# Delta rule units: inverse and masked blocks in the other half of the partitions, both updates' products in turn

## The chip, the core and the metric

The kernel runs on one core of one Trainium2 chip. A core has a matrix engine (TensorE, PE in the profile, with its weight loads as PEld), VectorE (DVE), ScalarE (ACT), GpSimd (POOL) and SyncE (SP), which issues the DMAs here. Each engine works through its own queue in order, and semaphores tie the queues together. The metric is the device time of one execution in microseconds (us), the median of several.

## What is computed

The reference runs two kinds of transformer blocks, two layers of each, on 512 tokens of width 1024, all in float32. What matters here is the delta rule of the first kind: 8 heads, chunks of 64 tokens, in both directions of time. For each head, direction and chunk it inverts a unit triangular 64x64 matrix:

```python
decay = jnp.exp(jnp.where(incl, gcum[..., :, None] - gcum[..., None, :], -jnp.inf))
k_beta = k * beta[..., None]
a_kk = jnp.where(strict, jnp.einsum("bhnid,bhnjd->bhnij", k_beta, k) * decay, 0.0)
eye = jnp.eye(c, dtype=q.dtype)
t_inv = lax.linalg.triangular_solve(eye + a_kk, jnp.broadcast_to(eye, a_kk.shape),
                                    left_side=True, lower=True, unit_diagonal=True)
u = jnp.einsum("bhnij,bhnjd->bhnid", t_inv, v * beta[..., None])
w = jnp.einsum("bhnij,bhnjd->bhnid", t_inv, k_beta * jnp.exp(gcum)[..., None])
```

A scan over the 8 chunks then carries a 64x64 state per head. Around it lie projections, grid attention, gates and a feed-forward network; the second kind of block has three other attention branches.

## The kernel before

The program is written five times over, once for each engine (classes Tensor, Scalar, Vector, Pool, Sync), with methods of the same names. Each method is a generator; `mixed` interleaves the generators in a fixed order, so that each engine's queue holds the delta rule's steps with other work (attention, projections, gates: the fill) between them. `up` marks a step as done on a semaphore, `at` names it for a wait. PSUM has eight banks, handed out in turn by `take` and put back by `give`, which says which steps must be over before the next user.

The delta rule's work is cut into units (l, g, jp, r): layer, group of four heads, pair of heads, direction. The two directions r = 0 and r = 1 run abreast, so a block (l, g, jp) holds two units, and there are eight blocks. A unit covers two heads and eight chunks, which is sixteen 64x64 matrices. They lie in tiles of 128 partitions by 512 elements: chunk parity a picks the partition half (64a to 64a + 63), and (head, pair of chunks) picks one of eight column blocks. Each r has five such tiles of s_xb: X, Y, Pm, A, AT.

TensorE's `eight` (L608) forms sixteen products of 64x64, one for each a and column block; half a of the operands gives half a of the result. `mm` (L517) is the line under which nearly all matmuls appear. A float32 product shows as two matmuls.

A unit runs as follows (Tensor L885, Vector L2252, Pool L2682).

- Gates, the products k k and q k (L915), masks; VectorE forms A (L2277) and the masked q k (L2282).
- TensorE transposes A to AT (L923), ScalarE copies it to s_xb.
- GpSimd masks: Pm from A (step X1, L2699), block C(1) from AT (L2705), Y from AT (step Y1, L2708), then C(2) to C(5), each one round ahead of its use. The C lie in three s_tmp tiles.
- VectorE forms the first inverse X = I - Pm (L2286) and its transpose Y = I - Y (L2288).
- Rounds b = 1 to 5 double the size of the inverted blocks: P = C x X on TensorE (L932), copied by ScalarE to Pm; then, for b < 5, all sixteen products of X's update (L939), then the sixteen of Y's (L942); VectorE subtracts each from X and Y (L2297, L2303). Round 5 updates Y only.
- u and w (L947 to L955): u = Y x value rows, w = A x Y. In w and in the products k k and q k the two inner loops run over all four pairings of an operand half with a result half.

On TensorE a round is: P of r = 0, P of r = 1, a step of fill or none, X and Y of r = 0, X and Y of r = 1, a step of fill or none. After both blocks of a group comes the chain over the chunks.

Of the kernel before, what the change touches and what calls it, by code (L numbers as in the profile page):

```python
# [37 lines left out]
M_ID = 14  # L38
# [74 lines left out]
def v8(a):  # L113
    return a.rearrange("p (b n) -> p b n", b=8)
# [399 lines left out]
class Tensor(Program):  # L514
# [90 lines left out]
            last = self.e.transpose(ps[:, i * 128:(i + 1) * 128], src[:, i * 128:(i + 1) * 128], self.m.cst[:, K_ID, :])  # L605
        return last

    def eight(self, ps, left, right):  # L608

        for b in range(8):  # L610
            for a in range(2):
                pr, s = slice(64 * a, 64 * a + 64), slice(b * 64, (b + 1) * 64)
                last = self.mm(ps[pr, s], left[pr, s], right[pr, s] if right is not None else self.m.cstm[pr, M_ID, :], True, True)
        return last

# [266 lines left out]

    def unit(self, l, g, jp, r):  # L885

        m, sc = self.m, self.m.sc
        X, Y, Pm, A, AT = m.slot[r]
        key, both = (l, g, jp, r), (l, g, jp)
# [30 lines left out]
        yield  # L920
        ps = self.take((key, "AT"))
        self.w.wait_ge(*self.at("vec_unit", key, "A", 1))
        self.eight(ps, A, None).then_inc(*self.up("pe_unit", key, "AT"))  # L923
        self.give((key, "AT"), ("act_unit", key, "AT"))
        yield
        yield
        for b in range(1, 6):
            C = self.tmp((key, "C", b))
            ps = self.take((key, "P", b))
            self.w.wait_ge(*self.at("pool_unit", key, "C", b))  # L930
            self.w.wait_ge(*self.at("vec_unit", key, "X", b - 1))
            self.eight(ps, C, X).then_inc(*self.up("pe_unit", key, "P", b))  # L932
            self.give((key, "P", b), ("act_unit", key, "P", b))
            yield
            self.w.wait_ge(*self.at("act_unit", key, "P", b))
            self.w.wait_ge(*self.at("vec_unit", key, "Y", b - 1))
            if b < 5:
                ps = self.take((key, "X", b))
                self.eight(ps, Y, Pm).then_inc(*self.up("pe_unit", key, "X", b))  # L939
                self.give((key, "X", b), ("vec_unit", key, "X", b))  # L940
            ps = self.take((key, "Y", b))
            self.eight(ps, Pm, Y).then_inc(*self.up("pe_unit", key, "Y", b))  # L942
            self.give((key, "Y", b), ("vec_unit", key, "Y", b))
            yield
        ps = self.take((key, "u"))
# [1001 lines left out]
class Vector(Program):  # L1947
# [304 lines left out]
    def unit(self, l, g, jp, r):  # L2252
# [29 lines left out]
            self.tt(m.M2[:, r, jp, s], X[:, s], self.bank((both, "kq", e))[:, 256:512], ALU.mult).then_inc(*self.up("vec_unit", key, "q", e))  # L2282
        yield
        self.w.wait_ge(*self.at("vec_unit", key, "q", 1))
        self.w.wait_ge(*self.at("pool_unit", key, "X1"))
        self.tt(v8(X), ident, v8(Pm), ALU.subtract).then_inc(*self.up("vec_unit", key, "X", 0))  # L2286
        self.w.wait_ge(*self.at("pool_unit", key, "Y1"))
        self.tt(v8(Y), ident, v8(Y), ALU.subtract).then_inc(*self.up("vec_unit", key, "Y", 0))  # L2288
        yield
        for b in range(1, 6):  # L2290
# [374 lines left out]
class Pool(Program):  # L2665
# [5 lines left out]
    def run(self):  # L2671
        m = self.m
        self.slots = [(b, ()) for b in m.cs]
        for l in range(2):
            self.w.wait_ge(*self.at("vec_qk", (l, "q", 4), "out"))
            self.w.wait_ge(*self.at("dma_spill", l))
            self.w.wait_ge(*self.at("dma_csta"))
            for g in range(2):
                together(self.units(l, g, 0), self.units(l, g, 1))
                self.chain(l, g)  # L2680

    def unit(self, l, g, jp, r):  # L2682
# [5 lines left out]
        if jp == 1:  # L2688
            heads = lambda a: a.rearrange("p i (h e) -> p i h e", h=4)
            hs = slice(8 * r + 4 * g, 8 * r + 4 * g + 4)  # L2690
            self.w.wait_ge(*self.at("act_proj", (l, "p", g, 1, 1), "tok"))
            self.w.wait_ge(*self.at("act_dn", (l, "bd"), "kd"))
            self.tt(heads(m.kdec[:, r]), heads(m.ktok[g][:, :, :]), B(sc["kd"][:, hs, :].rearrange("p c i -> p i c")[:, :, :, None], 3, 64), ALU.mult).then_inc(*self.up("pool_unit", key, "kdec"))
        yield
        yield
        yield
        yield
        self.w.wait_ge(*self.at("vec_unit", key, "A", 1))
        self.tt(v8(Pm), v8(A), over(MTT), ALU.mult).then_inc(*self.up("pool_unit", key, "X1"))  # L2699
        yield  # L2700

        def block(b):
            C = self.take((key, "C", b))
            self.w.wait_ge(*self.at("act_unit", key, "AT"))
            self.tt(v8(C), v8(AT), over(MT + b), ALU.mult).then_inc(*self.up("pool_unit", key, "C", b))  # L2705
            self.give((key, "C", b), ("pe_unit", key, "P", b))
        block(1)
        self.tt(v8(Y), v8(AT), over(MT), ALU.mult).then_inc(*self.up("pool_unit", key, "Y1"))  # L2708
        yield
        for b in range(1, 6):  # L2710
            if b < 5:
# [9 lines left out]
    def chain(self, l, g):  # L2721
        m = self.m
        key = (l, g)
        self.w.wait_ge(*self.at("act_dn", (l, "bd"), "egt"))
        for s in range(8):
            for r in range(2):
                c = s if r == 0 else 7 - s
                self.w.wait_ge(*self.at("vec_chain", key, "S", s - 1, r))
                self.tt(m.S[:, r, :, 64:128], m.S[:, r, :, 0:64], B(m.egt[:, c % 2, r, 2 * g:2 * g + 2, c // 2:c // 2 + 1], 2, 64), ALU.mult).then_inc(*self.up("pool_chain", key, s, r))


class Sync(Program):
# [183 lines left out]
```

## Time and profile before

| | us |
|---|---|
| runs | 3445.08, 3446.06, 3454.87 |
| median | 3446.06 |
| profiled execution | 3454.78 |
| its span | 3453.0 |
| TensorE busy | 3298.4 |
| VectorE busy | 1882.4 |
| ScalarE busy | 1437.2 |
| GpSimd busy | 200.7 |

The page gives busy time per engine, the busy share in 40 slices of the span (86 us each), the DMA queues, the chain of work that ended last, and the costliest groups of instructions. A matmul's duration in the trace is that of one pass through a pipeline, and several are under way at once: their pace shows in the distances between groups.

### The profile page before, as it was taken

What the parts mean: (1) busy time and instruction counts of PE and PEld (TensorE: products, weight loads), DVE (VectorE), ACT (ScalarE), POOL (GpSimd) and SP (SyncE); (2) the same over time, 40 slices, a digit from 0 to 9 for tenths busy, and PEclk for the clock granted to TensorE, in tenths of its full rate; (3) what the DMA queues carried; (4) which work ended last, traced back from release to release, by engine and by line L of the source; (5) the groups of instructions that cost most, each with busy time, mean ns of one, the idle gap of its engine ahead of it and who ended that gap; (6) DMA issues with size and microseconds to landing.
All of it is one profiled execution on the core that took longest, in us unless ns stands there. A gap on an engine that the chain in (4) does not pass through costs nothing.

```text
span 3453.0 us, 61428 instructions
## 1 busy us (share of the span) xinstructions
PE 3298.4 (96%) x26780; PEld 2625.2 (76%) x26780; DVE 1882.4 (55%) x2834; ACT 1437.2 (42%) x2518; POOL 200.7 (6%) x188
## 2 busy tenths in 40 slices
PE   8899999999998999999999998989999999999999
PEld 6587887788875787878788876767788767677787
DVE  6565657756565565557755654453444644434444
ACT  5534224434255443234433454444433445444432
POOL 0041330000000232300000000000000000000000
PEclk9999999999999999999999998999999999999999
DMA  4001103232331011123223231201122312111222
GB/s 153 25 21 45 39 27 123 93 104 92 97 113 49 8 33 50 33 69 117 92 95 101 81 118 47 95 30 63 55 89 78 109 48 89 44 58 59 78 73 95
DMA packets 75212, 249.15 MB, mean 72 GB/s; under 512 B 9280, under 2 KB 10944, under 8 KB 73920
## 3 DMA queue, kind: packets, MB, share of 16 engines
q1 hardware_dynamic: 74944, 245.22, 21.7%
q8 instruction: 212, 3.47, 0.4%
q14 instruction: 56, 0.46, 0.0%
HBM read 237.88 MB, written 6.29 MB: 71 GB/s over the span
## 4 chain that ended last, share of the span: by engine, by line
PE 85%; DVE 7%; ACT 6%; issue 2%; DMA 0%; SPq 0%; ACTq 0%; DVEq 0%
PE psum L518 82%; PE psum L695 2%; ACT s_tmp L1247 1%; ACT s_w L1247 1%; DVE s_nm L2033 1%; DVE s_tmp L1954 1%; DVE s_ffy L1954 1%; DVE s_w L1951 1%; ACT s_E L1247 1%; DVE s_tmp L1951 1%; ACT L1247 0%; DVE s_xb L1951 0%; PE psum L605 0%; ACT L1259 0%; ACT s_ffy L1247 0%
## 5 line engine op out<-in xcount | busy, mean ns | idle before, releaser
L518 PE MATMUL psum<-s_h,s_w 128*128 128x512 f32 (+1 forms) x6864 | 1665.3, 399 | 30.5 <-DVE s_tmp L1954 18.0
L518 PEld LDWEIGHTS psum<-s_h,s_w 128*128 128x128 f32 (+1 forms) x6864 | 1288.0, 190 | 337.4 <-issue 46.5
L1951 DVE TENSOR_TENSOR s_w<-s_stage,s_w 128x1024 fp32r<-128x1024 f32 (+2 forms) x468 | 530.1, 1134 | 410.5 <-ACT s_w L1247 408.8
L1247 ACT ACTIVATE s_w<-s_stage 128x1024 fp32r<-128x1024 f32 (+2 forms) x468 | 451.3, 966 | 284.4 <-PE psum L518 263.4
L518 PE MATMUL psum<-s_ffa,s_w 128*128 128x512 f32 x1056 | 242.1, 390 | 4.6 <-DVE s_ffa L1951 4.6
L518 PEld LDWEIGHTS psum<-s_ffa,s_w 128*128 128x128 f32 x1056 | 197.8, 188 | 47.9 <-DVE s_ffa L1951 7.1
L518 PE MATMUL psum<-s_oR,s_w 128*128 128x512 f32 (+1 forms) x960 | 211.5, 371 | 0.0
L2033 DVE TENSOR_REDUCE s_nm<-psum 128x1 f32<-128x512 f32 (+3 forms) x288 | 138.2, 521 | 126.8 <-PE psum L518 126.2
L1247 ACT ACTIVATE s_E<-psum,s_nm 128x256 f32<-128x256 f32 (+3 forms) x224 | 114.3, 515 | 192.8 <-DVE s_nm L2033 192.8
L1954 DVE SCALAR_TENSOR_TENSOR s_ffy<-psum,s_pcol,s_ffy 128x511 f32<-128x511 f32 x176 | 131.7, 748 | 111.3 <-ACT s_ffy L1247 108.2
L1247 ACT ACTIVATE s_tmp<-psum 128x512 f32<-128x512 f32 (+2 forms) x154 | 87.5, 568 | 244.5 <-PE psum L518 239.3
L518 PEld LDWEIGHTS psum<-s_oR,s_w 128*128 128x128 f32 x960 | 166.0, 189 | 29.2
L518 PE MATMUL psum<-s_raw,s_w 128*128 128x512 f32 (+1 forms) x720 | 173.2, 400 | 8.2 <-DVE s_raw L1954 8.2
L518 PEld LDWEIGHTS psum<-s_xb 64*64 64x64 f32 x5632 | 160.7, 135 | 14.5 <-issue 8.4
L518 PEld LDWEIGHTS psum<-s_raw,s_w 128*128 128x128 f32 (+1 forms) x720 | 133.0, 185 | 45.6 <-issue 12.7
L518 PE MATMUL psum<-s_xb 64*64 64x64 f32 x5632 | 166.0, 219 | 0.0
L1951 DVE TENSOR_TENSOR s_xb<-s_xb,psum 128x512 f32<-128x512 f32 (+1 forms) x176 | 107.5, 634 | 90.8 <-PE psum L518 89.9
L1247 ACT ACTIVATE s_xb<-psum 128x512 f32<-128x512 f32 x116 | 68.4, 597 | 165.9 <-PE psum L518 165.9
L1954 DVE SCALAR_TENSOR_TENSOR s_x<-psum,s_x 128x512 f32<-128x512 f32 x80 | 55.2, 690 | 144.9 <-PE psum L518 144.8
L1247 ACT ACTIVATE s_ffy<-psum,s_pcol 128x512 f32<-128x512 f32 x88 | 60.5, 687 | 168.1 <-PE psum L518 152.3
L2669 POOL TENSOR_TENSOR s_tmp<-s_xb,s_cstm 128x512 f32<-128x512 f32 x80 | 117.7, 1481 | 159.7 <-PE psum L518 154.2
L518 PE MATMUL psum<-s_tmp,s_cst 128*128 128x512 f32 (+2 forms) x184 | 82.9, 548 | 17.7 <-ACT s_tmp L1247 17.1
(284 smaller groups left out, 3491.2 us busy)
## 6 DMA issues: line engine op xcount, KB each, us to landing
s_stage<-w SPq DMA_DIRECT2D x192, 512.0 KB, 3.3
s_stage<-wup SPq DMA_DIRECT2D x88, 512.0 KB, 3.2
s_stage<-wo SPq DMA_DIRECT2D x32, 512.0 KB, 3.3
s_stage<-wdn SPq DMA_DIRECT2D x32, 512.0 KB, 3.5
s_stage<-wdn SPq DMA_DIRECT2D x16, 384.0 KB, 3.1
spill<-s_x SPq DMA_DIRECT2D x2, 2048.0 KB, 8.9
s_stage<-woa SPq DMA_DIRECT2D x16, 256.0 KB, 2.7
s_x<-spill SPq DMA_DIRECT2D x2, 2048.0 KB, 7.9
```

What stands on the lines that cost most here:

```text
L518: return self.e.matmul(out, left, right, start=first, stop=last, skip_group_check=True)
L695: last = self.e.transpose(ps[:, tile(c)], f.e(U)[:, tile(c)], m.cst[:, K_ID, :])
L1247: return self.e.activation(out, src, func, **kw)
L1951: return self.e.tensor_tensor(out, a, b, op)
L1954: return self.e.scalar_tensor_tensor(out=out, in0=a, scalar=s, in1=b, op0=op0, op1=op1)
L2033: self.e.tensor_reduce(m.nm[:, U % 8:U % 8 + 1], self.bank((tag, "S", U))[:, 0:n], X_AX, ALU.max, negate=True).then_inc(*self.up("vec_attn ...
L2669: return self.e.tensor_tensor(out, a, b, op)
```

## The change

Products may now go crossed: half a of the operands gives half 1 - a of the result. `eight` gets a flag for it, and its inner statement becomes `one`. The transpose to AT and the products P go crossed; so AT and the C lie in the other half, and X with them, while A, Y and Pm stay. In rounds 1 to 4 X's product (crossed) and Y's (straight) alternate, one by one, into two banks taken together; X's semaphore is raised by the last but one of the 32 products, Y's by the last. GpSimd forms Pm and Y half by half, because input and output now lie in different partition halves: two instructions on 64 partitions each instead of one on 128. It waits for the end of each of its own instructions around these, and remembers its last instruction in `self.last` for that. VectorE waits for the second half in each case.

```diff
-    def eight(self, ps, left, right):
+    def eight(self, ps, left, right, crossed=False):
         for b in range(8):
             for a in range(2):
-                pr, s = slice(64 * a, 64 * a + 64), slice(b * 64, (b + 1) * 64)
-                last = self.mm(ps[pr, s], left[pr, s], right[pr, s] if right is not None else self.m.cstm[pr, M_ID, :], True, True)
+                last = self.one(ps, left, right, a, b, crossed)
         return last
+
+    def one(self, ps, left, right, a, b, crossed):
+        pr, s = slice(64 * a, 64 * a + 64), slice(b * 64, (b + 1) * 64)
+        to = slice(64 - 64 * a, 128 - 64 * a) if crossed else pr
+        return self.mm(ps[to, s], left[pr, s], right[pr, s] if right is not None else self.m.cstm[pr, M_ID, :], True, True)
...
-        self.eight(ps, A, None).then_inc(*self.up("pe_unit", key, "AT"))
+        self.eight(ps, A, None, True).then_inc(*self.up("pe_unit", key, "AT"))
...
-            self.eight(ps, C, X).then_inc(*self.up("pe_unit", key, "P", b))
+            self.eight(ps, C, X, True).then_inc(*self.up("pe_unit", key, "P", b))
...
             if b < 5:
-                ps = self.take((key, "X", b))
-                self.eight(ps, Y, Pm).then_inc(*self.up("pe_unit", key, "X", b))
+                px, py = self.take((key, "X", b)), self.take((key, "Y", b))
+                for n in range(8):
+                    for a in range(2):
+                        last = self.one(px, Y, Pm, a, n, True)
+                        if (n, a) == (7, 1):
+                            last.then_inc(*self.up("pe_unit", key, "X", b))
+                        last = self.one(py, Pm, Y, a, n, False)
+                last.then_inc(*self.up("pe_unit", key, "Y", b))
                 self.give((key, "X", b), ("vec_unit", key, "X", b))
-            ps = self.take((key, "Y", b))
-            self.eight(ps, Pm, Y).then_inc(*self.up("pe_unit", key, "Y", b))
+            else:
+                py = self.take((key, "Y", b))
+                self.eight(py, Pm, Y).then_inc(*self.up("pe_unit", key, "Y", b))
...
-        self.w.wait_ge(*self.at("pool_unit", key, "X1"))
+        self.w.wait_ge(*self.at("pool_unit", key, "X1", 1))
...
-        self.w.wait_ge(*self.at("pool_unit", key, "Y1"))
+        self.w.wait_ge(*self.at("pool_unit", key, "Y1", 1))
...
-        self.tt(v8(Pm), v8(A), over(MTT), ALU.mult).then_inc(*self.up("pool_unit", key, "X1"))
+        if self.last is not None:
+            self.w.wait_ge(*self.at(*self.last))
+        for a in range(2):
+            self.tt(v8(Pm)[half(1 - a)], v8(A)[half(a)], over(MTT)[half(a)], ALU.mult).then_inc(*self.up("pool_unit", key, "X1", a))
+            self.w.wait_ge(*self.at("pool_unit", key, "X1", a))
...
-        self.tt(v8(Y), v8(AT), over(MT), ALU.mult).then_inc(*self.up("pool_unit", key, "Y1"))
+        self.w.wait_ge(*self.at("pool_unit", key, "C", 1))
+        for a in range(2):
+            self.tt(v8(Y)[half(a)], v8(AT)[half(1 - a)], over(MT)[half(1 - a)], ALU.mult).then_inc(*self.up("pool_unit", key, "Y1", a))
+            self.w.wait_ge(*self.at("pool_unit", key, "Y1", a))
```

## Rows read from the trace of the kernel before

**Rows 1.** The page: busy time by engine, GpSimd by slices, the chain.
```profile
PE 3298.4 (96%) x26780; PEld 2625.2 (76%) x26780; DVE 1882.4 (55%) x2834; ACT 1437.2 (42%) x2518; POOL 200.7 (6%) x188
...
POOL 0041330000000232300000000000000000000000
...
PE 85%; DVE 7%; ACT 6%; issue 2%; DMA 0%; SPq 0%; ACTq 0%; DVEq 0%
```

**Rows 2.** Busy us by stretch: PE, PEld, DVE, ACT, POOL, clock, DMA share, GB/s.
```profile
165.00:190.00 25.00, 22.06 (x260) 17.18 (x258) 17.88 (x32) 12.29 (x26) 9.75 (x7) 0.93 0.07 23
190.00:232.00 42.00, 42.00 (x1043) 36.71 (x1042) 23.41 (x37) 15.34 (x32) 12.81 (x9) 1.00 0.01 3
...
436.00:454.00 18.00, 15.99 (x239) 13.12 (x237) 14.82 (x20) 7.04 (x12) 11.27 (x8) 1.00 0.18 59
454.00:482.00 28.00, 28.00 (x700) 24.96 (x698) 12.83 (x18) 5.73 (x9) 9.18 (x7) 1.00 0.07 22
```

**Rows 3.** Timeline, TensorE, one round b: start, duration, engine, line, tiles, [idle before].
```profile
190.12 2.08 PE L518 MATMUL psum<-s_xb,s_tmp 64*64 64x64 f32 x64
192.14 1.13 PE L518 MATMUL psum<-s_vtok,s_dno 64*128 64x512 f32 x4
193.19 3.95 PE L518 MATMUL psum<-s_xb 64*64 64x64 f32 x128
197.07 1.09 PE L518 MATMUL psum<-s_ktok,s_vtok 128*64 128x128 f32 x16
...
199.12 2.08 PE L518 MATMUL psum<-s_xb,s_tmp 64*64 64x64 f32 x64
```

**Rows 4.** Tile s_xb: one group's durations min/median/max in ns, first and last start.
```profile
L518 PE MATMUL psum<-s_xb x5632: 217/218/268, 193.2 to 1481.2; 64*64 64x64 f32 x195
```

**Rows 5.** Timeline, TensorE: the k, q products; u and w of both r.
```profile
170.49 1.16 PE L518 MATMUL psum<-s_qkv 64*64 64x64 f32 x64
...
232.92 3.02 PE L518 MATMUL psum<-s_xb 64*64 64x64 f32 x128
```

**Rows 6.** First set-up, timeline of GpSimd and TensorE; then tile s_xb's VectorE group.
```profile
175.47 2.49 POOL L2669 TENSOR_TENSOR s_xb<-s_xb,s_cstm 128x512 f32<-128x512 f32 x2 [175.03 <-DVE s_xb L1951]
...
177.70 3.48 PE L518 MATMUL psum<-s_cstm,s_xb 64*64 64x64 f32 x64 [2.94 <-DVE s_x L1951]
...
180.38 1.27 POOL L2669 TENSOR_TENSOR s_tmp<-s_xb,s_cstm 128x512 f32<-128x512 f32 x1 [2.41 <-ACT s_xb L1247]
...
182.87 2.28 POOL L2669 TENSOR_TENSOR s_tmp<-s_xb,s_cstm 128x512 f32<-128x512 f32 x1
...
L1951 DVE TENSOR_TENSOR s_xb<-s_cstm,s_xb x32: 676/1764/1780, 186.4 to 1442.5; 128x512 f32<-128x512 f32 x32
```

**Rows 7.** Timeline, VectorE: an instruction and one that waits for it.
```profile
166.04 0.64 DVE L1951 TENSOR_TENSOR s_xb<-psum,s_scgc 128x512 f32<-128x512 f32 x1
...
166.72 0.69 DVE L1954 SCALAR_TENSOR_TENSOR s_xb<-s_xb,s_sclnb 128x512 f32<-128x512 f32 x1
```

**Rows 8.** Timeline of the third block's set-up: VectorE, GpSimd, TensorE's second P.
```profile
385.67 6.82 DVE L1951 TENSOR_TENSOR s_xb<-s_cstm,s_xb 128x512 f32<-128x512 f32 x4
386.86 1.74 POOL L2669 TENSOR_TENSOR s_xb<-s_xb,s_cstm 128x512 f32<-128x512 f32 x1
388.55 1.72 POOL L2669 TENSOR_TENSOR s_tmp<-s_xb,s_cstm 128x512 f32<-128x512 f32 x1
...
390.96 1.15 PE L518 MATMUL psum<-s_xb,s_tmp 64*64 64x64 f32 x32 [0.58 <-DVE s_xb L1951]
```

**Rows 9.** Timeline, TensorE: the transposes to AT of the fourth block.
```profile
441.73 2.08 PE L518 MATMUL psum<-s_cstm,s_xb 64*64 64x64 f32 x64 [2.01 <-DVE s_xb L1951]
```

**Rows 10.** Timeline of two rounds with nothing between Y and the next P.
```profile
455.74 3.95 PE L518 MATMUL psum<-s_xb 64*64 64x64 f32 x128
...
456.93 0.69 DVE L1951 TENSOR_TENSOR s_xb<-s_xb,psum 128x512 f32<-128x512 f32 x1 [1.19 <-PE psum L518]
...
459.52 2.03 PE L518 MATMUL psum<-s_xb,s_tmp 64*64 64x64 f32 x64
...
461.38 3.90 PE L518 MATMUL psum<-s_xb 64*64 64x64 f32 x128
461.60 0.60 ACT L1247 ACTIVATE s_xb<-psum 128x512 f32<-128x512 f32 x1 [0.34 <-PE psum L518]
```

More of the change, by code:

```diff
@@ L2673, in run @@
         self.slots = [(b, ()) for b in m.cs]
+        self.last = None
         for l in range(2):
@@ L2693, in unit @@
             self.tt(heads(m.kdec[:, r]), heads(m.ktok[g][:, :, :]), B(sc["kd"][:, hs, :].rearrange("p c i -> p i c")[:, :, :, None], 3, 64), ALU.mult).then_inc(*self.up("pool_unit", key, "kdec"))
+            self.last = "pool_unit", key, "kdec"
         yield
@@ L2698, in unit @@
         self.w.wait_ge(*self.at("vec_unit", key, "A", 1))
-        self.tt(v8(Pm), v8(A), over(MTT), ALU.mult).then_inc(*self.up("pool_unit", key, "X1"))
+        if self.last is not None:
[3 more added lines that the diff above has]
+            self.w.wait_ge(*self.at("pool_unit", key, "X1", a))
+        self.last = "pool_unit", key, "X1", 1
         yield
@@ L2705, in block @@
             self.tt(v8(C), v8(AT), over(MT + b), ALU.mult).then_inc(*self.up("pool_unit", key, "C", b))
+            self.last = "pool_unit", key, "C", b
             self.give((key, "C", b), ("pe_unit", key, "P", b))
         block(1)
-        self.tt(v8(Y), v8(AT), over(MT), ALU.mult).then_inc(*self.up("pool_unit", key, "Y1"))
+        self.w.wait_ge(*self.at("pool_unit", key, "C", 1))
+        for a in range(2):
+            self.tt(v8(Y)[half(a)], v8(AT)[half(1 - a)], over(MT)[half(1 - a)], ALU.mult).then_inc(*self.up("pool_unit", key, "Y1", a))
+            self.w.wait_ge(*self.at("pool_unit", key, "Y1", a))
         yield
@@ L2729, in chain @@
                 self.tt(m.S[:, r, :, 64:128], m.S[:, r, :, 0:64], B(m.egt[:, c % 2, r, 2 * g:2 * g + 2, c // 2:c // 2 + 1], 2, 64), ALU.mult).then_inc(*self.up("pool_chain", key, s, r))
+        self.last = "pool_chain", key, 7, 1
 class Sync(Program):
```

## The prediction

> **What bounds the kernel now.** The page comes first: TensorE is busy 96% of the span and holds 85% of the chain of work that ended last [rows 1]. GpSimd works in two short stretches only, slices 3 to 5 and 15 to 17; these are the stages of the delta rule, once per layer, and only they are touched. Next the busy time by stretches: inside the loops over b TensorE is busy in every microsecond at full granted clock, 42.00 of 42.00 and 28.00 of 28.00 [rows 2]. The stretches before these loops, the set-ups (masks, transposes, first inverse), are not full: 22.06 of 25.00 and 15.99 of 18.00. So a microsecond taken from TensorE in a loop is a microsecond of the kernel as long as nobody else gets late, and a microsecond added on GpSimd or VectorE in a set-up counts only past its cover.
>
> The timeline of one round b [rows 3] shows: the two products P (r = 0, 1) for 2.02 us start to start, an attention score 1.05, then the updates X and Y of both r, 128 matmuls in 3.88, then attention again, next P 9.00 us after the first. TensorE pauses nowhere.
>
> **What four quarters give.** Each float32 product of 64x64 is two matmuls in the trace. One takes 217 to 218 ns whatever surrounds it [rows 4], so the pace must be read from starts. All products of X, of Y and of P pair row half a with output half a: two quarters of the array in turn. 128 of them are 3.95 us busy; less the 0.22 that the last one lasts, the starts lie within 3.73, 29.15 ns each [rows 3]. The trace of before also has products that go through all four quarters in turn: the k, q products (L915: e inner, a outer), 64 matmuls in 1.16 us busy where P's 64 need 2.08. Less 0.22 that is 0.94, 14.7 each. And 232.92 is u (two quarters) and w (four quarters) of both r, 128 matmuls: 3.02 - 0.22 = 2.80, less 64 x 29.15 ns = 1.87 leaves 0.93 for w's 64, 14.6 each [rows 5]. The change puts X crossed and Y straight in turn: quarters (0,1), (0,0), (1,0), (1,1), all four before one comes again. I take 14.6 ns. Bounds: 14.6 (the rows with four) and 29.15 (the rows with two).
>
> The gain: X and Y of both r are 128 matmuls; 128 x (29.15 - 14.6) = 1.86 us per round. There are 4 rounds (b = 1 to 4) in each of 8 blocks (2 layers, 2 g, 2 jp), 32 in all: 59.6 us. Round 5 has only Y and stays; P and the transpose to AT go crossed but keep two quarters and their pace: crossed alone has no row, its bounds are the two-quarter price and, if crossing costs nothing, zero; I take zero.
>
> What the Trainium skill says against it: TensorEngine Tiling (Array Packing), "Restrictions and Gotchas", states that different row tiles can't use one PSUM bank at the same time; X's bank now gets products of both row halves, and so does Y's. By that page X and Y would stay at 29 ns and the gain would be nil. The trace disagrees for two: X before already writes one bank from both row halves, and its matmuls still come two per 58 ns. The k, q and w products put each row half in a bank of its own, so four at once with shared banks is not shown; hence a rival below.
>
> **GpSimd's set-up.** Pm (X1) and Y's start (Y1) change partition half, which takes two instructions each on 64 partitions instead of one on 128, and every one is followed by a wait for its own end. No row has a GpSimd instruction on 64 partitions. Bounds: half of 1.25 us, and 1.25 itself (2.49 for two [rows 6]). VectorE takes 0.69 us for 512 elements and 0.60 to 0.69 start to start: time goes by elements per partition, which the halves keep; I take 1.25. After a wait for its own engine VectorE starts 0.04 us behind the end of the instruction waited for: 166.04 + 0.64, then 166.72 [rows 7]. GpSimd's neighbours without a wait already overlap by 0.07 (2.49 for two of 1.28); I take 0.1 per wait, bounds 0 and 0.3.
>
> GpSimd's order in a set-up is X1(r0) X1(r1) C1(r0) Y1(r0) C1(r1) Y1(r1) C2(r0), so C1(r1) gets three more in front, Y1(r1) is over four later. GpSimd and VectorE also hold each other up: VectorE's instructions on s_cstm, s_xb take 0.68 alone and 1.76 beside GpSimd, GpSimd's on C1(r1) 2.28 instead of 1.27 beside VectorE's weight split [rows 6]; where both have work, one of each costs about 1.74 [rows 8]. VectorE forms X(r0), Y(r0), X(r1), Y(r1) in order, each waiting for GpSimd; P(r1) waits for X(r1), and the X,Y products of r1 for Y(r1).
> First block of a layer: GpSimd idles 2.41 us after X1, waiting for AT [rows 6]; this absorbs most of 2 x 1.25 + 0.4. C1(r1) ends at about 187.3 instead of 185.1, and from there the engines alternate: X(r0) by 188.3, Y(r0) by 190.0, X(r1) by 192.1. P(r1), half of P's 2.02 behind 190.12, could start at 191.1 [rows 3]. Loss 1.1 us; Y(r1), done by 194.1, is hidden by the first half of XY.
> Third block (g = 1, jp = 0), the dearest: TensorE waits already, 0.58 for X(r1), and the alternation fills VectorE from 385.7 to 392.5 [rows 8]. Three more GpSimd instructions in front of C1(r1) are 4 to 5 us, less 0.3 of idle; X(r1) needs only X1 and Y1(r0) and comes 0.8 later. Y1(r1), four later, ends at about 394.8, Y(r1) at 395.6, where the products of r1 want it at 393.6: 0.8 + 2.0 = 2.8.
> The second and fourth have the third's alternation, but TensorE reaches their P without waiting: I take 1.45 for each, the middle of 1.1 and 2.8 rounded down.
> Sum 6.8 per layer, 13.6 us in all. Cheapest case: halves at half price, 0 to 2 in all. Dearest: four instructions at 1.73 and twelve waits at 0.2, 9.3 per block with no cover, 74 us. My value is near the low end since TensorE has fill (12 to 36 large matmuls) in front of P. A stall of 1 to 2 us shouldn't lower TensorE's clock: a wait of 2.01 left the next 64 matmuls at 2.08 us, with that stretch granted 1.00 (2.4 GHz), while after 2.94 they took 3.48, part of them at the 1.2 GHz level, in a stretch granted 0.93 [rows 2, 6, 9]. Behind VectorE's longer wait for Y1(r1) stand copies out of PSUM, convolution sums and weight splits of the fill; the products that need them come in the next round, and a round is 9 us: at nothing, at most another 1 us a block if that cover fails.
>
> **The later X.** X's last product is now the last but one of 32, so X(r) and Y(r) come together, 0.93 us per r. VectorE needs 4 x 0.69 = 2.76 for all four, from 1.19 us after the start of XY (455.74, 456.93). With attention or projections behind XY (1.65 to 3 us) P finds all of it done. In 4 rounds of each layer P follows at once, as at 459.52 [rows 10]. There: X(r0) ends at 1.19 + 0.69 = 1.88, P(r0) starts at about 2.0 for 1.87; X(r1) ends at 1.19 + 2.07 = 3.3, P(r1) starts at 3.4 for 2.9. Loss 0.6, eight times: 4.8 us. Taking both banks at once asks for Y's bank 0.93 us earlier; banks are given back rounds before, nothing. ScalarE's copy of P(r1) ends 461.60 + 0.60, 0.82 us after XY starts at 461.38 [rows 10], and will be wanted at 0.93: just hidden.
>
> **The sum.** -59.6 + 13.6 + 4.8 = -41.2 us. Against the profiled execution (span 3453.0, 3454.78 in all) 3413.6. That execution lies 8.7 us above the median, 3446.06; from the median it is 3404.9, say 3405.
>
> **Rivals.**
> A, forecast: 14.6 ns per matmul, small stalls; own range 3387 (all 59.6 kept) to 3423 (set-ups at 4 us a block). 0.77.
> B, GpSimd's chain replaces TensorE as the bound of the set-ups. It decides at (59.6 - 4.8) / 8 = 6.9 us lost per block: beyond, the kernel is slower. Between 4 and 6.9 it eats the gain, 3423 to 3446; at 9.3 it gives 3446 - 59.6 + 4.8 + 74 = 3465. For it: no idle on GpSimd in three of four set-ups, TensorE already waits in the third. Against: the fill in front of P, and TensorE needs only part of the seven masks. 0.11: 0.02 still faster, 0.05 within, 0.04 slower.
> C, four quarters don't run beside each other when both row halves share the banks: each bank takes one row half at a time and XY keeps its 3.88. No gain, the later X does no harm at that pace, the 13.6 of the set-ups remain: 3460, slower by 0.4%. For it: no row with four quarters and shared banks. Against it: the pairs in X now share a bank. It decides as soon as XY keeps more than 3.5 us (13.6 / 32 = 0.43 gained per round pay the set-ups). 0.07. The page named above would bring this about.
> D, a pace in between, as 21.9 ns, the middle of the bounds: 4096 x 7.25 ns = 29.7 gained, 18.4 lost, 3435; at 24.7 ns nothing is left. Against: both rows with four quarters keep 14.6. 0.05, of it 0.02 faster.
> By TensorE: Matmul & The Clock Gate of the Trainium skill, section "Wait — 56ns, not 53.3ns?", starts are never nearer than about 25 ns, which would give D at its end, 3447. The trace disagrees, with 64 starts in 0.94 us [rows 5].
>
> **Chances.** 0.3% of 3446, about 10 us, is what a measurement can tell from no change. Faster: A 0.77, B 0.02, D 0.02, together 0.81. Within: B 0.05 and D 0.03, 0.08. Slower: C 0.07 and B 0.04, 0.11. The range that holds 8 in 10: A's, and B and D up to 3437, so 3387 to 3437.
>
> **What would show it.** Right: XY groups of 128 matmuls fall from 3.88 to about 2.0 us start to start, and the round of 9.00 to 7.1; P stays at 2.02; GpSimd shows eight instructions of 64 partitions at 1.25 in each set-up; waits for VectorE's s_xb of 1 to 3 us appear on TensorE around the first P of each block and of 0.5 in the rounds with P behind XY. Wrong: XY at 3.9 (C) or near 3 (D), GpSimd instructions of 64 partitions over 1.8 us or waits over 7 us a block (B). It is wrong too if VectorE, busy 56% of a round stretch today [rows 2], or ScalarE fall behind the shorter rounds and leave gaps on TensorE all through the loops.

## The result

| | before | after |
|---|---|---|
| median, us | 3447.32 (3444.21 to 3456.79) | 3437.47 (3432.89 to 3442.00) |
| profiled execution | 3454.78 | 3437.19 |
| its span | 3453.0 | 3435.4 |
| TensorE busy | 3298.4 | 3252.9 |
| GpSimd busy | 200.7 | 253.8 |

The ratio over all runs is 0.9966, 95% interval [0.9957, 0.9974]: 11.7 us faster (9 to 15; the two medians lie 9.9 apart), just over what a measurement tells from no change. The forecast was 3405, a gain of 41; the time lies 0.5 us above the end of the range and in the middle of rival B's. The sign was right, under a third of the gain came. The two profiled executions differ by 17.6, more than the medians, because that of before lay above its median; so the traces are compared by place, and sizes are taken from ratios.

The page of the kernel after: busy time by engine, GpSimd by slices, the chain that ended last by engine and by line. Its lines are shifted: L1951 is L1964, L1954 is L1967, L1247 is L1260, L2669 is L2682.
```profile
PE 3252.9 (95%) x26780; PEld 2575.1 (75%) x26780; DVE 1886.2 (55%) x2834; ACT 1437.4 (42%) x2518; POOL 253.8 (7%) x220
...
POOL 0051330000000332500000000000000000000000
...
PE 80%; DVE 9%; ACT 6%; POOL 3%; issue 2%; DMA 0%; SPq 0%; POOLq 0%; ACTq 0%; DVEq 0%
```
GpSimd was absent from this chain before [rows 1]; now it holds 3% of the span, VectorE 2% more, TensorE 5% less.

Timeline of TensorE in a round of the first block, after (start, duration, engine, line, tiles):
```profile
206.52 2.08 PE L518 MATMUL psum<-s_xb,s_tmp 64*64 64x64 f32 x64
208.53 1.13 PE L518 MATMUL psum<-s_vtok,s_dno 64*128 64x512 f32 x4
209.59 2.10 PE L518 MATMUL psum<-s_xb 64*64 64x64 f32 x128
211.62 1.09 PE L518 MATMUL psum<-s_ktok,s_vtok 128*64 128x128 f32 x16
212.64 1.09 PE L700 MATMUL psum<-s_cst,s_x 128*128 128x128 f32 x8
213.67 1.55 PE L518 MATMUL psum<-s_xb,s_tmp 64*64 64x64 f32 x45
```
The 128 matmuls of X and Y take 2.10 busy, 2.03 start to start, where they took 3.88 [rows 3]; P keeps 2.01, the round falls from 9.00 to 7.15. The step that carried the forecast is right: (2.10 - 0.22) / 128 = 14.7 ns per matmul, where 14.6 was taken. So the loss is elsewhere.

Timeline of TensorE after, second block of layer 0 (to 263), then the third and the fourth, then the fourth of layer 1. In brackets the idle time before and who ended it:
```profile
249.95 1.15 PE L518 MATMUL psum<-s_xb,s_tmp 64*64 64x64 f32 x32
253.15 1.83 PE L518 MATMUL psum<-s_xb,s_tmp 64*64 64x64 f32 x29 [2.06 <-DVE s_xb L1964]
...
257.58 3.01 PE L518 MATMUL psum<-s_h,s_w 128*128 128x512 f32 x12
263.00 3.47 PE L518 MATMUL psum<-s_xb,s_tmp 64*64 64x64 f32 x64 [2.41 <-DVE s_xb L1964]
```
```profile
383.52 1.15 PE L518 MATMUL psum<-s_xb,s_tmp 64*64 64x64 f32 x32
386.88 1.05 PE L518 MATMUL psum<-s_xb,s_tmp 64*64 64x64 f32 x29 [2.22 <-DVE s_xb L1964]
...
390.08 1.16 PE L518 MATMUL psum<-s_xb 64*64 64x64 f32 x64 [1.11 <-DVE s_xb L1964]
391.17 1.66 PE L518 MATMUL psum<-s_h,s_w 128*128 128x512 f32 x6
394.66 2.73 PE L518 MATMUL psum<-s_xb,s_tmp 64*64 64x64 f32 x64 [1.82 <-DVE s_xb L1964]
...
456.33 2.76 PE L518 MATMUL psum<-s_xb,s_tmp 64*64 64x64 f32 x61 [2.41 <-DVE s_xb L1964]
```
```profile
1435.11 1.15 PE L518 MATMUL psum<-s_xb,s_tmp 64*64 64x64 f32 x32 [1.57 <-DVE s_xb L1964]
...
1442.27 2.25 PE L518 MATMUL psum<-s_xb,s_tmp 64*64 64x64 f32 x61 [2.40 <-DVE s_xb L1964]
```
The second block of layer 0 waits 4.5 us, the third 5.2, the fourth 2.4 (its 1.99 before AT stood there before, [rows 9]); before, the third had 0.58 [rows 8]. There is a second wait, at P of round 2 (263.00, 394.66, 456.33), which the prediction had put at nothing. Behind these three waits P takes 3.47, 2.73 and 2.76 instead of 2.08. That is not the clock alone: P of r = 1 also has to wait for its own X, and in the fourth block of layer 1 (1442.27), where the granted clock was 1.00, it takes 2.25.

Busy us by stretch, 50 us each from the k,q products of the second, third and fourth block of each layer: PE, PEld, DVE, ACT, POOL, granted clock (1.00 is the 2.4 GHz level all through, a part at 1.2 GHz lowers it), DMA share, GB/s. The kernel before, then after:
```profile
242.00:292.00 50.00, 49.13 (x936) 42.09 (x928) 34.78 (x46) 24.22 (x36) 21.16 (x14) 1.00 0.14 44
...
sum 300.00, PE 293.11 PEld 255.38 DVE 191.43 ACT 105.49 POOL 130.73; mean PE 48.85 PEld 42.56 DVE 31.90 ACT 17.58 POOL 21.79
```
```profile
236.00:286.00 50.00, 44.96 (x848) 37.54 (x840) 35.20 (x44) 21.66 (x33) 28.19 (x18) 0.93 0.14 44
370.00:420.00 50.00, 44.26 (x1075) 36.95 (x1074) 29.95 (x39) 14.17 (x23) 30.68 (x20) 0.97 0.14 45
431.00:481.00 50.00, 45.45 (x1100) 38.74 (x1099) 29.55 (x41) 15.31 (x24) 26.30 (x18) 0.93 0.10 34
1221.00:1271.00 50.00, 45.14 (x875) 38.05 (x872) 36.18 (x44) 20.47 (x31) 28.14 (x18) 0.93 0.13 44
1357.00:1407.00 50.00, 44.81 (x1106) 37.92 (x1106) 30.70 (x41) 13.66 (x23) 30.69 (x20) 0.97 0.14 45
1417.00:1467.00 50.00, 43.94 (x1118) 37.07 (x1118) 30.33 (x42) 15.32 (x24) 26.26 (x18) 1.00 0.10 35
sum 300.00, PE 268.56 PEld 226.28 DVE 191.91 ACT 100.59 POOL 170.26; mean PE 44.76 PEld 37.71 DVE 31.98 ACT 16.77 POOL 28.38
```
Before, TensorE is idle for 300 - 293.1 = 6.9 us and the granted clock is 1.00 in all six. After, it is idle for 31.4, and the clock shortfalls add up to 0.27 x 50 = 13.5 us. Together 38 us more lost than before, in set-ups for which the prediction had put down 13.6.

The waits for s_xb, added up over both layers, say where: in round 1 they are 11.2 us longer than before, at P of round 2 13.1 us. The first blocks show none. The whole traces agree: the span fell by 17.6 us, TensorE's busy time by 45.5 where the faster quarters alone take out 59.2, so 13.7 us of busy time came back, and its idle time rose by 27.9. Nor is the clock that of one execution: over the whole kernel it was 0.979 to 0.984 in the ten runs after, and 0.983 to 0.987 in the 35 runs of the kernel before that stand beside the experiments.

The chain behind the third block's waits, after: GpSimd, then VectorE.
```profile
379.14 2.15 POOL L2682 TENSOR_TENSOR s_tmp<-s_xb,s_cstm 128x512 f32<-128x512 f32 x1
381.38 2.96 POOL L2682 TENSOR_TENSOR s_xb<-s_xb,s_cstm 64x512 f32<-64x512 f32 x2
384.42 1.77 POOL L2682 TENSOR_TENSOR s_tmp<-s_xb,s_cstm 128x512 f32<-128x512 f32 x1
386.26 2.94 POOL L2682 TENSOR_TENSOR s_xb<-s_xb,s_cstm 64x512 f32<-64x512 f32 x2
389.29 5.15 POOL L2682 TENSOR_TENSOR s_tmp<-s_xb,s_cstm 128x512 f32<-128x512 f32 x3
```
```profile
384.38 2.36 DVE L1964 TENSOR_TENSOR s_xb<-s_cstm,s_xb 128x512 f32<-128x512 f32 x2 [2.53 <-POOL s_xb L2682]
389.24 0.69 DVE L1964 TENSOR_TENSOR s_xb<-s_cstm,s_xb 128x512 f32<-128x512 f32 x1 [2.50 <-POOL s_xb L2682]
389.85 3.46 DVE L1964 TENSOR_TENSOR s_xb<-s_ktok,s_scbgc 128x512 f32<-128x512 f32 x2
```
GpSimd works almost without a gap from C(1) of r = 0 to the second half of Y of r = 1: 379.14 to 389.20, 10.1 us. VectorE, which before worked through its four instructions in one run [rows 8], now stands still for 2.53 and 2.50 us, waiting for the two Y, and X of r = 1 is stuck behind the first. Then it forms the key rows for w at 1.73 each, beside GpSimd's C(2), and only after that subtracts X and Y of round 1, which P of round 2 wants.

So three reasons compete. Theory 1: the chain of masks with half instructions on GpSimd (rival B). Theory 1a: VectorE's queue, the order X, Y, X, Y, key rows. Theory 2: the shorter rounds lose by themselves, since X is raised late.

### The profile page after: what moved, and what is told of

It is laid out like the page before. It is cut to its first block, busy times and chain, and to the rows that moved or that the text cites. A ratio compares the mean times of both kernels' runs of the same rounds, so it can differ in the third digit from the quotient of the medians.

```text
span 3435.4 us, 61486 instructions
## 1 busy us (share of the span) xinstructions
PE 3252.9 (95%) x26780; PEld 2575.1 (75%) x26780; DVE 1886.2 (55%) x2834; ACT 1437.4 (42%) x2518; POOL 253.8 (7%) x220
## 3 DMA queue, kind: packets, MB, share of 16 engines
q8 instruction: 212, 3.47, 0.4%
## 4 chain that ended last, share of the span: by engine, by line
PE 80%; DVE 9%; ACT 6%; POOL 3%; issue 2%; DMA 0%; SPq 0%; POOLq 0%; ACTq 0%; DVEq 0%
PE psum L518 77%; PE psum L700 2%; POOL s_xb L2682 2%; DVE s_xb L1964 1%; ACT s_tmp L1260 1%; DVE s_tmp L1967 1%; ACT s_w L1260 1%; DVE s_nm L2046 1%; DVE s_ffy L1967 1%; DVE s_w L1964 1%; POOL s_tmp L2682 1%; ACT s_E L1260 1%; ACT L1260 1%; DVE s_tmp L1964 1%; ACT L1272 0%
## 5 line engine op out<-in xcount | busy, mean ns | idle before, releaser
L1964 DVE TENSOR_TENSOR s_w<-s_stage,s_w 128x1024 fp32r<-128x1024 f32 (+2 forms) x468 | 528.6, 1130 | 414.5 <-ACT s_w L1260 412.8
L1260 ACT ACTIVATE s_w<-s_stage 128x1024 fp32r<-128x1024 f32 (+2 forms) x468 | 451.3, 966 | 285.3 <-PE psum L518 263.5
L1260 ACT ACTIVATE s_E<-psum,s_nm 128x256 f32<-128x256 f32 (+3 forms) x224 | 114.5, 516 | 191.4 <-DVE s_nm L2046 191.4
L1967 DVE SCALAR_TENSOR_TENSOR s_ffy<-psum,s_pcol,s_ffy 128x511 f32<-128x511 f32 x176 | 131.7, 748 | 110.0 <-ACT s_ffy L1260 106.9
L1260 ACT ACTIVATE s_tmp<-psum 128x512 f32<-128x512 f32 (+2 forms) x154 | 87.7, 569 | 243.1 <-PE psum L518 237.9
L2682 POOL TENSOR_TENSOR s_xb<-s_xb,s_cstm 64x512 f32<-64x512 f32 x64 | 92.5, 1446 | 927.5 <-DVE s_xb L1964 923.1
L1260 ACT ACTIVATE s_xb<-psum 128x512 f32<-128x512 f32 x116 | 68.4, 597 | 161.9 <-PE psum L518 161.8
L1967 DVE SCALAR_TENSOR_TENSOR s_x<-psum,s_x 128x512 f32<-128x512 f32 x80 | 55.3, 691 | 144.9 <-PE psum L518 144.8
L1964 DVE TENSOR_TENSOR s_xb<-s_xb,psum 128x512 f32<-128x512 f32 (+1 forms) x176 | 101.2, 630 | 57.5 <-PE psum L518 57.5
L1260 ACT ACTIVATE s_ffy<-psum,s_pcol 128x512 f32<-128x512 f32 x88 | 60.5, 687 | 166.7 <-PE psum L518 151.0
L2682 POOL TENSOR_TENSOR s_tmp<-s_xb,s_cstm 128x512 f32<-128x512 f32 x80 | 121.1, 1528 | 103.3 <-PE psum L518 101.4
L518 PEld LDWEIGHTS psum<-s_xb 64*64 64x64 f32 x5632 | 106.1, 138 | 20.3 <-ACT s_xb L1260 10.5
L518 PE MATMUL psum<-s_xb 64*64 64x64 f32 x5632 | 113.4, 224 | 6.3 <-issue 2.9
```

Source lines behind the costliest of these rows:

```text
L518: return self.e.matmul(out, left, right, start=first, stop=last, skip_group_check=True)
L1260: return self.e.activation(out, src, func, **kw)
L1964: return self.e.tensor_tensor(out, a, b, op)
L1967: return self.e.scalar_tensor_tensor(out=out, in0=a, scalar=s, in1=b, op0=op0, op1=op1)
L2682: return self.e.tensor_tensor(out, a, b, op)
```

## Experiments

### Halves without crossing

The kernel before with GpSimd's half instructions and waits for itself, all straight:
```diff
-        self.tt(v8(Pm), v8(A), over(MTT), ALU.mult)...
+        for a in range(2):
+            self.tt(v8(Pm)[half(a)], v8(A)[half(a)], over(MTT)[half(a)], ALU.mult)...
+            self.w.wait_ge(*self.at("pool_unit", key, "X1", a))
```
and Y likewise.

> The kernel before with GpSimd's two set-up steps in halves and its waits for its own end, but nothing crossed and X and Y in their old order. Theory 1 (the price of the change is the longer GpSimd set-up: +4 instructions a block, and what VectorE and TensorE then wait for): 20 to 45 us over before, ratio 1.006 to 1.013, with waits of TensorE for VectorE's s_xb around the first P of each block. Theory 2 (the halves are cheap, and the gain is lost because the shorter rounds leave VectorE behind): 0 to 5 us over before, ratio 1.000 to 1.0015.

Measured: 3474.43 beside 3452.25, ratio 1.0067 [1.0051, 1.0082], 23 us slower. The halves cost 2.9 us a block even with TensorE at its old pace and its longer rounds, where the prediction had 1.7. TensorE's waits for s_xb rise from 2.6 to 8.3 us in each layer.

### Crossing with whole masks

The changed kernel with GpSimd's X1 and Y1 whole and straight and no waits for itself. The first X and Y then lie in the wrong halves: the inverse is not computed, the work of the other engines is the same.
```diff
-        for a in range(2):
-            self.tt(v8(Pm)[half(1 - a)], v8(A)[half(a)], over(MTT)[half(a)], ALU.mult)...
+        self.tt(v8(Pm), v8(A), over(MTT), ALU.mult)...
```


> The changed kernel with GpSimd's two set-up steps whole again (one instruction on 128 partitions each, no waits for its own end). Pm and Y then start in the wrong half, so the inverse isn't computed; all other work is there. Theory 1: nearly all of the 59.6 us shows, 3385 to 3400 us, ratio 0.983 to 0.987. Theory 2: 3430 to 3437, as the changed kernel.

Measured: 3408.30, ratio 0.9879 [0.9862, 0.9896], 42 us faster. Taking the halves away gives back 30 of the missing us. 18 of the 59.6 are missing still.

### The key rows later

The changed kernel with VectorE's key rows for w formed in round 3:
```diff
-            if b == 1:
+            if b == 3:
                 self.w.wait_ge(*self.at("act_proj", (l, "p", g, 1, 1), "tok"))
                 self.tt(e4(A), tok(m.ktok[g]), each4("bgc"), ALU.mult)...
```


> The changed kernel with VectorE's product of key rows and decay (s_xb from s_ktok, needed only by w at a block's end) moved from round 1 to round 3, out of the time in which GpSimd catches up. Theory 1a (TensorE's wait for X at the P of round 2, 2.2 to 2.8 us and a lower clock after it, comes from these two instructions, 3.3 us beside GpSimd): that wait is gone or below 0.5, 10 to 25 us under the changed kernel, 3412 to 3427. Theory 1b (VectorE is late there anyway, from its wait for the second half of Y1): the wait stays near 2, 3432 to 3437.

Measured: 3418.47, ratio 0.9913 [0.9895, 0.9931]. Repeated later beside other kernels:

> The changed kernel with the key rows for w in round 3 once more, beside the others on the same chip: 0.9913 [0.9895, 0.9931] before. If it holds, 0.990 to 0.993; the difference to the version with C(1) on VectorE is what the GpSimd chain costs.

3417.92, ratio 0.9904 [0.9888, 0.9919]. So 18 to 21 us of the missing gain hang on two VectorE instructions per block (one for each r) that the change did not touch. The waits for s_xb fall from 14.0 to 7.6 us in layer 0, and the one at P of round 2 is gone. Were they dear before as well? The kernel before with the same one edit:

> The kernel before with one edit: VectorE forms the key rows for w (A from s_ktok and s_scbgc) in round 3 instead of round 1. If the move pays only where GpSimd's half instructions make VectorE late (my theory), nothing changes: 0.998 to 1.001. If the move would pay in any kernel, then the 19 us that it gave the changed kernel were no part of the change's cost: 0.994 to 0.996.

Measured: ratio 1.0009 [1.0000, 1.0018]: no gain, if anything a loss of 3 us. The rows became dear through the change.

### Crossing on VectorE

GpSimd's masks whole; VectorE writes the first X and Y crossed, in two instructions on 64 partitions each:
```diff
-        self.tt(v8(X), ident, v8(Pm), ALU.subtract)...
+        for a in range(2):
+            self.tt(v8(X)[half(1 - a)], ident[half(a)], v8(Pm)[half(a)], ALU.subtract)...
```
(Y likewise, out of A, into which GpSimd's Y1 goes.)

> The changed kernel with the crossing of halves given to VectorE: GpSimd masks whole tiles in place of the halves (Pm, and Y's start into A), VectorE forms the first X and Y by two instructions on 64 partitions each, reading one half and writing the other. GpSimd has its seven instructions again, VectorE four more of 0.69 us. Theory 1 (the length of GpSimd's queue sets the loss): 3400 to 3415, ratio 0.987 to 0.991. Rival (any four more instructions in the alternation of the two engines cost the same): 3430 to 3440.

Measured: 3423.83, ratio 0.9927 [0.9903, 0.9951], 25 us faster, less than expected. With late key rows as well:

> GpSimd's masks whole (no half instructions, no waits for itself), VectorE crosses the first X and Y in two half instructions each, and the key rows for w are formed in round 3. The crossing on VectorE alone stood at 0.9927 and the late key rows took 19 us from the changed kernel. If those 19 us came from VectorE's queue being late at P of rounds 1 and 2 whoever does the crossing, this one reaches 0.986 to 0.989. If they came only from GpSimd's share of the port, it stays at 0.990 to 0.993.

Measured: 3426.83, ratio 0.9936 [0.9922, 0.9950]: nothing gained by the move. VectorE's row in its third block, and the group's durations (minimum, median, maximum in ns) over the kernel, show what bounds this version:
```profile
378.00 9.35 DVE L1964 TENSOR_TENSOR s_xb<-s_cstm,s_xb 64x512 f32<-64x512 f32 x8
...
L1964 DVE TENSOR_TENSOR s_xb<-s_cstm,s_xb x64: 676/687/1779, 187.7 to 1429.3; 64x512 f32<-64x512 f32 x64
```
Eight halves take 9.35 us where four whole ones took 6.82 [rows 8]. At its shortest a half takes 676 ns, as a whole one did (676 to 1780, [rows 6]): half as many partitions do not make an instruction cheaper on VectorE either. Their mean of 1.17 us lies under the 1.7 of the four because GpSimd is done before the last of them; beside it they take up to 1779 ns too. The chain is nearly as long as GpSimd's 10.1. And the late key rows, worth 18 to 21 us with the crossing on GpSimd, have nothing to give here: TensorE's long wait stands at P of round 1 (3.5 us in the third block), and already with early key rows P of round 2 waited 0.4 us at most.

### Both X first

The changed kernel with late key rows, VectorE forming both first X and one step later both first Y, GpSimd masking C(1) of both r and then the two Y:
```diff
         self.tt(v8(X), ident, v8(Pm), ALU.subtract)...
-        self.w.wait_ge(*self.at("pool_unit", key, "Y1", 1))
-        self.tt(v8(Y), ident, v8(Y), ALU.subtract)...
         yield
         for b in range(1, 6):
+            if b == 1:
+                self.w.wait_ge(*self.at("pool_unit", key, "Y1", 1))
+                self.tt(v8(Y), ident, v8(Y), ALU.subtract)...
```


> The changed kernel with its GpSimd halves and waits kept, key rows for w in round 3, and the set-up in another order: VectorE forms both first X one after the other and both first Y one step later; GpSimd masks C(1) of both directions and then the two Y. If the missing gain is the chain GpSimd half instructions, VectorE's first Y of r = 0, first X of r = 1, P of r = 1 (theory 1), P's waits for s_xb in the set-ups fall from 14 us in layer 0's stretch to under 5 and the ratio is 0.986 to 0.990, near the 0.9879 of the kernel without half instructions. If GpSimd's half instructions themselves bound the set-up (rival B), or if the loss sits in the rounds, it stays at 0.990 to 0.993.

Measured: 3428.74, ratio 0.9946 [0.9932, 0.9960], 11 to 14 us worse than the kernel with late key rows alone and above both ranges that I had expected. TensorE in its third block, then GpSimd:
```profile
385.32 2.08 PE L518 MATMUL psum<-s_xb,s_tmp 64*64 64x64 f32 x64
388.65 1.16 PE L518 MATMUL psum<-s_xb 64*64 64x64 f32 x64 [1.24 <-DVE s_xb L1964]
393.18 1.98 PE L518 MATMUL psum<-s_xb 64*64 64x64 f32 x64 [3.37 <-DVE s_xb L1964]
```
```profile
384.84 2.94 POOL L2683 TENSOR_TENSOR s_xb<-s_xb,s_cstm 64x512 f32<-64x512 f32 x2
387.86 1.78 POOL L2683 TENSOR_TENSOR s_tmp<-s_xb,s_cstm 128x512 f32<-128x512 f32 x1
389.72 2.59 POOL L2683 TENSOR_TENSOR s_xb<-s_xb,s_cstm 64x512 f32<-64x512 f32 x2
```
P's wait is gone, as meant, and stands in front of X and Y instead, 4.6 us in all. They wait for the last Y of GpSimd, which is later by the C(2) that my order let in between (387.86, 1.78). So this run does not test VectorE's order X, Y, X, Y by itself: it also lengthened the way to the last Y. What it does show is that in both orders TensorE meets the end of GpSimd's chain, at P or at X and Y. This pointed to rival B.

### C(1) off GpSimd

If the chain bounds the set-up, shortening it must pay though the halves stay. VectorE, which stands still there, forms C(1) out of AT's bank; GpSimd goes from AT straight to Y. Key rows late:
```diff
         self.tt(v8(X), ident, v8(Pm), ALU.subtract)...
+        self.w.wait_ge(*self.at("pe_unit", key, "AT"))
+        self.after(self.k.tmp.get((key, "C", 1, "free"), ()))
+        self.tt(v8(self.tmp((key, "C", 1))), v8(self.bank((key, "AT"))), B(m.cstm[:, (M_MT if r == 0 else M_MTT) + 1, None, :], 1, 8), ALU.mult).then_inc(*self.up("vec_unit", key, "C1"))
...
-        block(1)
```
TensorE's first P waits for this C(1) instead of GpSimd's, and GpSimd's Y no longer waits for C(1) but for ScalarE's copy of AT only.

> The changed kernel with key rows for w in round 3, and the first masked block C(1) formed by VectorE out of AT's bank instead of by GpSimd out of AT's copy; the half instructions stay. GpSimd's chain after AT falls from C, Y, Y, C, Y, Y (10.1 us in the third block) to four halves (about 5.9), under the 6.5 us of the kernel before. If that chain bounds the set-ups (rival B of the prediction, and what the run with the first X and Y apart pointed to: there the wait only moved from P to X and Y), the waits for s_xb fall to under 1.5 us a block and the ratio comes to 0.986 to 0.989. If what is missing lies in VectorE's queue, which gets two instructions more here, it stays at 0.991 or above.

Measured: 3402.20 beside 3453.73, ratio 0.9860 [0.9840, 0.9879], 48 us faster than before: better than both kernels. TensorE in its third block; then the sum over the six stretches, for the version with late key rows alone and for this one:
```profile
377.48 1.15 PE L518 MATMUL psum<-s_xb,s_tmp 64*64 64x64 f32 x32
380.11 1.05 PE L518 MATMUL psum<-s_xb,s_tmp 64*64 64x64 f32 x29 [1.48 <-DVE s_tmp L1964]
...
381.06 2.07 PE L518 MATMUL psum<-s_xb 64*64 64x64 f32 x126
383.05 1.65 PE L518 MATMUL psum<-s_h,s_w 128*128 128x512 f32 x6
```
```profile
sum 300.00, PE 277.84 PEld 233.08 DVE 193.47 ACT 107.86 POOL 167.05; mean PE 46.31 PEld 38.85 DVE 32.24 ACT 17.98 POOL 27.84
...
sum 300.00, PE 286.83 PEld 241.84 DVE 200.72 ACT 114.08 POOL 151.53; mean PE 47.80 PEld 40.31 DVE 33.45 ACT 19.01 POOL 25.26
```
Waits in the third block fall from 5.2 us in the changed kernel and 3.3 with late key rows to 1.5, and what is left waits for the new C(1). Idle time in the six stretches goes from 31.4 by 22.2 to 13.2 us; the clock shortfall, 13.5 in the changed kernel, is 3 us (0.97 twice) in both of the others. Against the same kernel with C(1) on GpSimd, on the same chip, 0.9904 and 0.9860: 15 us by two masks a block moved from GpSimd to VectorE. VectorE's queue got longer, and the kernel faster. That decides between theories 1 and 1a for this part: it is the chain.

The same with early key rows:

> As the one before, but the key rows for w stay in round 1, as in the changed kernel. If those rows cost only where they run beside GpSimd's catching up (C(2) twice, behind the late half instructions), they cost little here, as in the kernel before (0.9 us gained there by the move): within 5 us of the one before. If they cost in themselves, some 19 us more, as between the changed kernel and its late version.

Measured: 3412.99, ratio 0.9894 [0.9874, 0.9913]: 12 us lost to the early rows (2 to 21), 25 won over the changed kernel by C(1) alone. Neither of the two outcomes expected: the rows cost about half of what they cost there. In layer 0 P of round 2 still waits, 2.04, 1.23 and 0.47 us. So theory 1a stands for a part that doesn't vanish with the chain.

### What the rounds lose

The kernel before with X and Y in turn into two banks, all straight:
```diff
-                ps = self.take((key, "X", b))
-                self.eight(ps, Y, Pm)...
+                px, py = self.take((key, "X", b)), self.take((key, "Y", b))
+                for n in range(8):
+                    for a in range(2):
+                        last = self.one(px, Y, Pm, a, n)
+                        ...
+                        last = self.one(py, Pm, Y, a, n)
```


> The kernel before with one edit: in rounds 1 to 4 X's and Y's products alternate into two banks taken together, as in the change, but all straight; GpSimd, AT and P as before. Two quarters of the array only, so a group of X and Y should keep its 29 ns a matmul (3.7 to 3.9 us x128). What it prices is the other part of the edit: X raised at the end of the group instead of its middle, and the banks taken together. By the prediction's own term this is 4.8 us, 0 to 8: ratio 1.000 to 1.002. The kernel with crossed products and whole masks left 17 us of the 59.6 missing; if that loss belonged to the later X alone, whatever the pace, it must show here: 1.004 to 1.006. If it comes only because the rounds are 1.9 us shorter and the work beside them no longer fits, this run shows next to nothing.

Measured: 3458.19, ratio 1.0017 [1.0006, 1.0028], 6 us slower (2 to 10).
```profile
195.91 4.00 PE L518 MATMUL psum<-s_xb 64*64 64x64 f32 x128
```
In two quarters the group keeps its pace (4.00, before 3.95 [rows 3]): it is the crossing that brings the second pair of quarters, not the turn. The later X costs about what was put down for it, 4.8.

The upper bound, whole masks (inverse not computed) and late key rows:

> The changed kernel with GpSimd's masks whole and straight (the first X and Y lie in the wrong halves, so the inverse is not computed) and the key rows for w in round 3. It bounds what the set-ups can give back: all that is missing to 59.6 us here is lost in the rounds. If the rounds lose it through X raised late and copies of P that no longer hide (my theory now), the late rows change nothing: 0.986 to 0.989, as without them 0.9879. If part of it was VectorE's queue at P of round 2, 0.984 to 0.986.

Measured: 3399.90, ratio 0.9852 [0.9836, 0.9868], 51 us faster. Without the late key rows whole masks had 0.9879, so the rows give 9 us here too (1 to 17), where I had expected nothing: about half of their 18 to 21 us comes with the shorter rounds, whatever GpSimd does. Of the 59.6, 8.5 are still missing (3 to 14). The set-ups of layer 0 wait for s_xb as before the change (2.9 us, before 2.6), so I put these 8.5 down to the rounds. One such place, TensorE and then ScalarE of this kernel:
```profile
279.84 1.02 PE L518 MATMUL psum<-s_tmp,s_cst 128*128 128x512 f32 x2
281.53 2.10 PE L518 MATMUL psum<-s_xb 64*64 64x64 f32 x128 [0.67 <-ACT s_xb L1260]
```
```profile
279.58 1.28 ACT L1272 ACT_TABLE_LOAD   x1
280.88 1.09 ACT L1260 ACTIVATE s_xb<-psum 128x512 f32<-128x512 f32 x2
```
The copies of P stand behind a table load of 1.28 us, and X and Y wait 0.67 us for them. The kernel before had this load too, and there nobody waited for the copies.

Not tried: the changed kernel without GpSimd's waits for its own instructions. What these waits cost by themselves is read from its trace only: four halves in 5.29 us at 175.74, when each takes 1.26 alone, so some 0.08 a wait.

## Why the prediction was wrong

Step by step, in us against the kernel before:

| step | predicted | measured | by |
|---|---|---|---|
| four quarters | -59.6 | -59.2 by the rows | XY 3.88 to 2.03 start to start, 32 rounds |
| rounds: later X, copies | +4.8 | +6 and +8.5 | in turn straight; whole masks, late rows |
| set-ups | +13.6 | +39 | 0.9966 against 0.9852 |
| of it waits in round 1 | +13.6 | +11.2 | traces |
| of it waits at P of round 2 | 0 | +13.1 | traces |
| of it clock | 0 | +13.5 | granted clock of six stretches |
| sum | -41 | -12 | |

**The quarters, and rivals C and D.** Right. The Trainium skill, TensorEngine Tiling (Array Packing), section "Restrictions and Gotchas", bars different row tiles from one PSUM bank at the same time; here both row halves write both banks in turn at 14.7 ns per matmul, so the measurement speaks against it. P and AT went crossed at no price, as taken.

**GpSimd's half instruction.** Right in size: 1.26 us alone, about 0.08 a wait, 2.6 to 3.5 for a pair in company.

**The set-ups.** This is the step that failed: 13.6 us were put down and 39 came, 4.9 a block, inside rival B's 4 to 6.9, which was given 0.11. What was priced was not the fault. The waits of round 1 came to 11.2. In the third block 2.8 was forecast and 2.22 - 0.58 + 1.11 = 2.75 measured, though divided otherwise: the wait for X of r = 1 grew by 1.64 instead of 0.8, the one for Y of r = 1 by 1.11 instead of 2.0. "TensorE needs only part of the seven masks" was wrong: it needs all but C(2), 10.1 us of chain against 6.5 before, behind a fill of 7 to 9 us. Two terms that I had put at nothing made the difference; with the waits of round 1 they come to 38 by the traces.
First, what stands behind VectorE's wait. I priced the wait by TensorE's next step alone. Behind it stood the key rows and the subtractions of round 1, and these were late for P of round 2: 1.8 to 2.4 us in six of eight blocks, 13.1 in all. I had listed copies, convolution sums and weight splits, not the key rows, and written "at nothing, at most another 1 us a block". The late key rows give back 18 to 21 us in the changed kernel and nothing in the one before; of that, 9 to 12 come with the shorter rounds even where GpSimd's chain is short.
Second, the clock. I took a wait of 1 to 2 us to be harmless, on one row with 2.01 [rows 9]. The changed kernel was granted 0.93 and 0.97 in five of six stretches: 13.5 us, as much as all that was put down for the set-ups. And the row itself was weak ground. The same wait in front of the same transposes stands in other versions too; here after, and in the version with C(1) on VectorE:
```profile
436.05 2.61 PE L518 MATMUL psum<-s_cstm,s_xb 64*64 64x64 f32 x64 [1.99 <-DVE s_xb L1964]
...
424.05 3.55 PE L518 MATMUL psum<-s_cstm,s_xb 64*64 64x64 f32 x64 [1.99 <-DVE s_xb L1964]
```
In both layers before and in layer 1 after they took 2.08. Nor does more waiting always lower the clock: the sixth stretch after has the most idle time, 6.06 us, and was granted 1.00. So the length of a wait alone does not decide. With late key rows, where the second wait is missing and the first (2.2 us in the third block) stays, the shortfall over the six stretches is 3 us (0.97 twice): the loss of clock came with the second waits. That they caused it is read from these rows, not tested by itself.

**ScalarE's copies "just hidden".** Wrong by a little: they hid in 0.93 us only where nothing stood in front of them. The rounds lost 8.5 us instead of 4.8, which the interval of 3 to 14 also allows.

**The other side.** The point at which B makes the kernel slower, 6.9 us a block, was not reached; with 4.9 lost and 1.1 in the rounds, 7.45 - 6.0 = 1.5 us a block are left, 12 us.

What stays open: which waits lower the clock and which do not, and how the 39 would divide if GpSimd's halves, the key rows and the clock could be changed one without the other. Taking the halves away gives 30 us with early key rows and 18 with late ones, so the shares depend on the order in which they are taken.

## What to carry to other kernels

When the fast part gets faster, every wait that was hidden behind its old pace comes due: price the chains beside it at the new pace, and for an instruction that now waits, list everything queued behind it to the next step that the bounding engine takes, not only the instruction itself. If two orders of a helper's queue only move the wait, the chain in front is too long; shorten it, or give a link to an engine that stands still there. And do not take a wait to be harmless to the clock from one row: look at the same place in other executions. Cutting an instruction in two by partitions doubled its cost on GpSimd and on VectorE here, so a change of partition half belongs where data pass through TensorE anyway.

## What was not expected of the hardware

- Four quarters with shared banks keep 14.7 ns per matmul, P and AT crossed keep 29 ns.
- VectorE on 64 partitions takes as long as on 128: 676 ns at the shortest for 512 elements either way; GpSimd too, 1.26 against 1.28 us.
- One and the same wait of 1.99 to 2.01 us was followed by 64 matmuls in 2.08, 2.61 or 3.55 us, in different executions and layers.
